# Splitting the copy of the selected key blocks between ScalarE and VectorE in a hybrid decoder step

## What is computed

```python
k_full = cache_k[page_table[:, :own_first]].astype(f32).reshape(Bd, n_full, MOBA_BLOCK, H, D)
kmean = jnp.mean(k_full, axis=2)
gate = jnp.einsum('bhtd,bnhd->bhtn', qf, kmean)
_, sel = lax.top_k(gate, topk)                      # 3 of 16 blocks, for each of 8 heads
...
s = jnp.einsum('bhtd,bhtkd->bhtk', qf, kg.astype(f32)) * scale
scores.append(s - slopes * (tpos[None, None, :, None] - kpos).astype(f32))
...
p = jax.nn.softmax(jnp.concatenate(scores, axis=-1), axis=-1)
```

## Time and profile before

| what | us |
|---|---|
| median of 3 runs | 459.38 |
| lowest and highest | 459.01 and 478.45 |
| the profiled execution's own time | 457.99 |
| span of the profile | 456.4 |

### The profile page before, as it was taken

The page is one execution under the profiler, slowest core; times in us unless marked ns, Lnnn a source line. Parts: engine busy times, 40 slices in busy tenths (PEclk is TensorE's granted clock), DMA queues, the critical chain, the costliest instruction groups (busy, mean ns, idle before and its releaser), DMA issues.

```text
span 456.4 us, 8864 instructions
## 1 busy us (share of the span) xinstructions
PE 402.1 (88%) x2696; PEld 189.5 (42%) x2696; DVE 278.8 (61%) x756; ACT 125.2 (27%) x282; POOL 244.7 (54%) x347
## 2 busy tenths in 40 slices
PE   4896997998779999899998897989999388999993
PEld 2543442433343444344553354434443253334433
DVE  2443167447624569666966884868865796567432
ACT  2310120000012223554547522362435401000101
POOL 4776305556446506563377745882566556667121
PEclk9897998999979999899999998999999769999999
DMA  8999158996799936997499849975699599945311
GB/s 223 408 390 337 49 183 227 363 328 164 202 382 331 254 105 190 361 320 185 117 336 318 241 127 333 327 202 156 210 368 337 162 362 378 343 103 117 115 46 52
DMA packets 79695, 111.26 MB, mean 244 GB/s; under 512 B 46560, under 2 KB 47584, under 8 KB 79648
## 3 DMA queue, kind: packets, MB, share of 16 engines
q0 software_dynamic: 22576, 71.45, 46.4%
q1 hardware_dynamic: 45280, 21.26, 18.3%
q10 hardware_dynamic: 11792, 17.98, 13.2%
HBM read 106.34 MB, written 4.29 MB: 242 GB/s over the span
## 4 chain that ended last, share of the span: by engine, by line
PE 27%; DMA 25%; issue 13%; POOL 10%; DVE 9%; SPq 7%; another core or an unknown queue 4%; DVEq 2%; POOLq 2%; ACT 1%
DMA K<-in_cache_k,kidx 20%; PE PA L1036 12%; POOL K L899 8%; PE PA L1142 7%; SPq L777 4%; DVE ksum L1619 4%; DMA V<-in_cache_v 2%; PE SB L990 2%; PE GB L1159 2%; DMA V<-in_page_table 2%; PE DC L1188 1%; DVEq L1617 1%; POOLq L726 1%; SPq L780 1%
## 5 line engine op out<-in xcount | busy, mean ns | idle before, releaser
L899 POOL DMA_INDIRECT K<-in_cache_k,kidx x128 | 135.5, 1059 | 135.3 <-DVE ksum L1619 69.2
L1036 PE MATMUL PA<-wbuf,hT 128*128 128x512 f32 x384 | 187.8, 623 | 4.5 <-ACT vn L1302 2.6
L744 DVE TENSOR_TENSOR ksum<-K 128x512 f32<-128x512 f32 x128 | 86.5, 689 | 74.7 <-DMA K<-in_cache_k,kidx 54.4
L1036 PEld LDWEIGHTS PA<-wbuf,hT 128*128 128x128 f32 x384 | 69.4, 196 | 82.1 <-issue 73.3
L729 POOL DMA_DIRECT2D V<-in_cache_v x128 | 76.2, 595 | 33.8 <-issue 26.1
L1142 PE MATMUL PA<-wbuf,hT 128*128 128x512 f32 x128 | 59.6, 606 | 0.0
L1619 DVE TENSOR_TENSOR ksum<-K,qb 128x128 f32<-128x128 f32 x192 | 41.8, 287 | 10.9 <-issue 4.3
L1159 PE MATMUL GB<-ksum,win 128*32 128x512 f32 x256 | 34.1, 604 | 5.0 <-DVE ksum L744 4.7
L1142 PEld LDWEIGHTS PA<-wbuf,hT 128*128 128x128 f32 x128 | 23.1, 192 | 25.7 <-issue 25.2
L1036 PE MATMUL PA<-hT,wbuf 128*128 128x512 f32 x64 | 31.0, 630 | 0.0
L990 PE MATMUL SB<-wbuf,hTs 128*32 128x128 f32 x576 | 22.0, 305 | 6.7 <-DMA wbuf<-in_w_in 3.7
(11 more groups left out here) (200 smaller groups left out, 363.5 us busy)
## 6 DMA issues: line engine op xcount, KB each, us to landing
wbuf<-in_w_in ACTq DMA_DIRECT2D x20, 512.0 KB
V<-in_cache_v SPq DMA_DIRECT2D x240, 32.0 KB
V<-in_cache_v POOLq DMA_DIRECT2D x128, 32.0 KB, 2.8
wbuf<-in_w_out ACTq DMA_DIRECT2D x8, 512.0 KB
wbuf<-in_w_in SPq DMA_DIRECT2D x8, 256.0 KB, 8.6
K<-in_cache_k,kidx POOLq DMA_INDIRECT x128, 7.8
wbuf<-in_w_in SPq DMA_DIRECT2D x4, 512.0 KB
qb<-q_rows SPq DMA_DIRECT2D x8, 256.0 KB
```

Source lines behind the costliest of these rows:

```text
L744: eng.tensor_tensor(ksum[:, n % SUMS, :], K[:, n, 0, :], K[:, n, 1, :], ALU.add).then_inc(s_dsum, 1)
L899: pool.indirect_dma_start(K[:, n, :, :].rearrange("p r w -> p (r w)"), None, k_rows, bass.IndirectOffsetOnAxis(ap=kidx[:, b, n:n + 1], axis=0)
L1036: last = pe.matmul(bank[:, :], lhs, rhs, start=(kc == 0), stop=(kc == KC - 1))
```

## The change

ScalarE gets a new step "ex", with the highest priority in its plan. It waits for `s_sel`, loads eight registers, and copies the eight blocks of rank one from `K` to `kq` without a product. It raises `s_exa`. VectorE keeps the 16 products of ranks two and three, in four parts of four. Then a new VectorE step "em" waits for `s_exa` and multiplies the eight copies in place by q, as one instruction of 128 partitions x 8 x 128 elements, and raises `s_exm`. `K` is free when both `s_ext` and `s_exa` are up; the q row's buffer `qb` is free when both `s_ext` and `s_exm` are up. The costs in the plan change with it, and `MARGIN` goes from 0.6 to 1.0.

```diff
-PARTS = 4
+PARTS, BY_ACT = 4, 8
...
-            deps = [("DVE", ("ex", b - 1, PARTS - 1))] if b else []
+            deps = [("DVE", ("ex", b - 1, PARTS - 1)), ("ACT", ("ex", b - 1))] if b else []
...
-            add("DVE", "gate", s, {"ex": 1.7, "pg": 1.2, "sr": 3.4}[s[0]], *deps)
+            if s[0] == "em":
+                deps.append(("ACT", ("ex", b)))
+            add("DVE", "gate", s, {"ex": 1.15, "pg": 1.2, "em": 1.2, "sr": 3.4}[s[0]], *deps)
+        add("ACT", "copyk", ("ex", b), 3.1, ("DVE", ("pg", b)))
...
-            add("SP", "spread", ("qb", b), 3.0, ("DVE", ("ex", b - 1, PARTS - 1)))
+            add("SP", "spread", ("qb", b), 3.0, ("DVE", ("em", b - 1)))
...
-TILE_US, KEY_US, LAG, MARGIN, SLACK, QUARTERS = 7.4, 1.65, 0.25, 0.6, 0.05, 8
+TILE_US, KEY_US, LAG, MARGIN, SLACK, QUARTERS = 7.4, 1.65, 0.25, 1.0, 0.05, 8
...
                     if b >= 1 and n == 0:
                         pool.wait_ge(s_ext, b)
+                        pool.wait_ge(s_exa, b)
...
+                elif kind == "ex":
+                    b = s[1]
+                    act.wait_ge(s_sel, b + 1)
+                    if b >= 1:
+                        act.wait_ge(s_scr, b)
+                    for x in range(BY_ACT):
+                        k, h = divmod(x, H)
+                        if h == 0:
+                            block_regs = [act.alloc_register(f"ablk{b}_{k}_{i}") for i in range(H)]
+                            act.load(block_regs, selT[k:k + 1, b % 2, 0:H])
+                        n = act.snap(block_regs[h], min_val=0, max_val=NB - 1)
+                        last = act.copy(kq[:, h * TOP + k, :, :],
+                                        K[:, bass.ds(n, 1), :, h * HD:(h + 1) * HD].rearrange("p a r d -> p (a r) d"))
...
+                    last.then_inc(s_exa, 1)
...
-                    size = H * TOP // PARTS
-                    for x in range(size * part, size * (part + 1)):
+                    size = (H * TOP - BY_ACT) // PARTS
+                    for x in range(BY_ACT + size * part, BY_ACT + size * (part + 1)):
...
+                elif kind == "em":
+                    b = s[1]
+                    dve.wait_ge(s_exa, b + 1)
...
+                        last = dve.tensor_tensor(by_rank[:, k, 0:hs, :, :], by_rank[:, k, 0:hs, :, :],
+                                                 q_heads[:, 0:hs, :].unsqueeze(2).broadcast_to([P, hs, 2, HD]),
+                                                 ALU.mult)
+                    last.then_inc(s_exm, 1)
                 elif kind == "sr":
                     b = s[1]
                     dve.wait_ge(s_ext, b + 1)
+                    dve.wait_ge(s_exm, b + 1)
```

More of the change, by code:

```diff
@@ L63, in add @@
         needs[eng, s] = deps
-    for eng, names in (("PE", "gate score first attention side sample project"), ("ACT", "weight square score exp turn sample side evacuate squares fetch"),
+    for eng, names in (("PE", "gate score first attention side sample project"), ("ACT", "copyk weight square score exp turn sample side evacuate squares fetch"),
                        ("DVE", "first " + DVE_LANES), ("POOL", POOL_LANES), ("SP", "spread rows fetch gather"),
@@ L270, in make_plan @@
         parts = [("ex", b, i) for i in range(PARTS)]
-        for s in ([("pg", b)] + parts if b == B - 1 else parts[:1] + [("pg", b)] + parts[1:]) + [("sr", b)]:
+        for s in ([("pg", b)] + parts if b == B - 1 else parts[:1] + [("pg", b)] + parts[1:]) + [("em", b), ("sr", b)]:
             deps = [("ACT", ("mb", b - 1))] if s[0] == "sr" and b else []
-            add("DVE", "gate", s, {"ex": 1.7, "pg": 1.2, "sr": 3.4}[s[0]], *deps)
+            if s[0] == "em":
+                deps.append(("ACT", ("ex", b)))
+            add("DVE", "gate", s, {"ex": 1.15, "pg": 1.2, "em": 1.2, "sr": 3.4}[s[0]], *deps)
+        add("ACT", "copyk", ("ex", b), 3.1, ("DVE", ("pg", b)))
         if b:
-            add("SP", "spread", ("qb", b), 3.0, ("DVE", ("ex", b - 1, PARTS - 1)))
+            add("SP", "spread", ("qb", b), 3.0, ("DVE", ("em", b - 1)))
         add("PE", "score", ("bc", b), 0.4, ("DVE", ("pg", b)), ("DVE", ("sr", b)))
@@ L592, in hymba_kernel @@
         s_scr = sem("selected_k_scored")
+        s_exa = sem("selected_k_copied")
+        s_exm = sem("copied_k_times_q")
         s_mxr = sem("decode_max_ready")
@@ L823, in _ @@
                         sp.wait_ge(s_ext, b)
+                        sp.wait_ge(s_exm, b)
                     sp.dma_start(qb[:, :], q_rows[b:b + 1, :].broadcast_to([P, W])).then_inc(s_qb, 16)
@@ L1353, in _ @@
                     fetch_v(act, b, hh, [k], "va")
+                elif kind == "ex":
[11 more added lines that the diff above has]
+                                        K[:, bass.ds(n, 1), :, h * HD:(h + 1) * HD].rearrange("p a r d -> p (a r) d"))
+                        if h == H - 1 or x == BY_ACT - 1:
+                            for r in block_regs:
+                                act.free_register(r)
+                    last.then_inc(s_exa, 1)
                 elif kind == "mb":
@@ L1628, in _ @@
                         last.then_inc(s_ext, 1)
+                elif kind == "em":
+                    b = s[1]
+                    dve.wait_ge(s_exa, b + 1)
+                    by_rank = kq[:, :, :, :].rearrange("p (h k) r d -> p k h r d", k=TOP)
+                    q_heads = qb[:, :].rearrange("p (h d) -> p h d", h=H)
+                    for k in range(-(-BY_ACT // H)):
+                        hs = min(H, BY_ACT - k * H)
+                        last = dve.tensor_tensor(by_rank[:, k, 0:hs, :, :], by_rank[:, k, 0:hs, :, :],
+                                                 q_heads[:, 0:hs, :].unsqueeze(2).broadcast_to([P, hs, 2, HD]),
+                                                 ALU.mult)
+                    last.then_inc(s_exm, 1)
                 elif kind == "sr":
```

2 lines of the change are left out of this document (1 added, 1 removed).

## The result

The changed kernel took 470.91 us (median of 4 runs, 469.13 to 475.71), the kernel before 460.03 beside it (459.01 to 478.45). The ratio is 1.026, with a 95% interval of 1.016 to 1.036. The forecast was 458.5 us, 446 to 467, with 12% for slower: the result lies outside. Single executions of either kernel scatter by 3% and more, and the ratios leave the disturbed ones out.

A forecast was written before the change was run, and what follows sets the result against it. TensorE and the key cycle were taken as two bounds within a few us. Terms -4.7 + 6.2 + 1.5 - 4.0 = -1.0 us took 457.99 to 457.0; 1.4 for the runs' median gave 458.4, rounded to 458.5, range 446 to 467.

The forecast's parts named there:

- The gaps: From each sequence's gate to the next first gather: 1.75 us shorter, or 0.7 at worst.
- The load stage as a constant: Sixteen gathers of a sequence, first to last: 25.0 us, taken as fixed within the key cycle of 46.3 us.
- ScalarE's hold: ScalarE held until 9.4 us after the gate, delaying copies out of TensorE's banks: costed at nothing, at worst 1 us a sequence.
- The tail: Time behind the last gate, 52.6 us before: longer by more TensorE steps (+6.2 us) and a later end (+1.5).
- seven more steps: TensorE behind the last gate: 47 projection steps against 40, +6.2 us.
- the longer end: Behind TensorE's last sample product: squaring, scaling and storing the prompt's last tile, +1.5 us (0 to 3).
- `MARGIN` gives back 4.0 us: TensorE's waits for key sums (4.7 us) and in one score step (4.2): larger `MARGIN` takes back 4 of 8.9 us.
- The stretches by numbers of steps: Stretches between gates, costed by TensorE's moved projection and attention steps and the keys' pace: -4.7 us to the last gate.
- The last stretch: Stretch to gate 7: output projection from about 21 us, 46 to 47 us against 48.2, so -1.5 us.
- B: Rival: the order costs more than the keys give; last gate no earlier, longer tail paid in full, 467 us; chance 0.13.
- C: Rival: ScalarE comes late with the copies, each delay moving the next load; 470 us, slower; chance 0.10.
- A: Rival: the key cycle sets the pace, so seven gaps each 1.75 us shorter count in full; 447 us; chance 0.22.

The follow-up runs named there:

- e2: Changed kernel's order with ScalarE's copies and "em" struck out, VectorE making all 24 products again; 477.49 us, ratio 1.030 to the kernel before.
- e1: Kernel before, its order kept, with only ScalarE's copies and "em" put in; 457.35 us against 463.96, ratio 0.987.
- e15: The kernel of e1 run once more, in five rounds; 461.90 us against 463.58 for the kernel before.
- e5: Changed kernel with only the four residual loads issued later, after the last sequence's gathers are issued; 467.81 us, ratio 1.010 to the kernel before.
- e8: The kernel of e1 with the four residual loads issued later, as in e5; 458.95 us against 465.95 for the kernel before.
- e9: Changed kernel with each weight chunk's four quarter loads issued together and the residual loads late; 466.80 us, ratio 1.009 to the kernel before.
- e16: The kernel of e1 with weight loads drawn together as in e9, but residual loads at their first place; two times, 458.42 and 472.67 us.
- e13: The changed kernel run again, nothing altered; 470.21 us against 463.58 for the kernel before, ratio 1.030.
- e3: Kernel before with only `MARGIN` raised from 0.6 to 1.0; 475.51 us against 463.96.
- e4: Changed kernel with `MARGIN` put back from 1.0 to 0.6; 494.75 us, ratio 1.071 to the kernel before.

## Why the prediction was wrong, point by point

- **The gaps: right.** Forecast 1.75 us less per sequence, the first gather 9.6 to 10.6 us after the gate. Measured -12.5 us in seven, 1.8 each, and 9.6 to 10.2 us in six of the seven gaps; the gap ahead of sequence 6 was 11.2 and 12.4 (13.2 and 13.0 before). The time of a copy (294 ns, forecast 0.30) and of "em" (1.22 us, forecast 1.23) were right too; only the copies overlap more than assumed.
- **The load stage as a constant: this step failed.** I took 25.0 us for every sequence out of one stretch and carried it over ("46.3 - 1.8 = 44.5"). It has no such value: it depends on what other queues move beside it. The rows for that stood in the trace of before, as the last stage took 26.5 us (367.66 to 394.13) with 3.3 MB beside it. I had costed ScalarE's hold as a matter of TensorE's banks, "at nothing", and forgot that the queue behind the copies holds the weight loads: of a step that holds an engine, every DMA behind it counts. Nor did I look where the new order puts the loads. The stages came to 26.9 us on the mean instead of 25.0: 13.6 us in seven, more than the whole gain, of which the order alone makes 5.7 (e2) and the copies alone 5 to 9 (e1, e15). So the key cycle that I put at 44.5 us stayed at 46.8 (10.2 + 26.9 + 9.7), where it had been. For the last stage (+5.8) e5, e8, e9 and e16 show that the bytes are the cause; for the other six (+7.8) it is the likely one.
- **The tail: right in kind, too large in size.** The terms were seven more steps (+6.2) and the longer end (+1.5), 7.7 us together; measured are +5.5, 58.1 and 58.0 us. TensorE's last product ends 51.1 us behind the gate instead of 46.3 (+4.8), and what follows takes 7.0 us instead of 6.3 (+0.6). The shorter gap does not show here: with the copies alone the tail is 52.5 us (e1), with the order alone 58.1 (e2).
- **`MARGIN` gives back 4.0 us: not so.** TensorE's wait for key sums, 4.7 us in the earlier trace rows, is 9.3 in the changed kernel and 7.5 in e13, and its waits for ScalarE's copy-out, 4.2 us there, are 5.0 and 4.0. In the kernel before the larger margin costs 11.5 us (e3), with the copies the smaller one costs about 24 (e4 against the changed kernel). I had priced a planner's constant by the waits it is aimed at; it reorders all, and has no sign of its own.
- **The stretches by numbers of steps:** to the last gate I had -4.7 and -4.0 us. The means of the last gate are 409.9 in both kernels, (403.8 + 415.9) / 2 and (411.5 + 408.3) / 2: nothing, as well as two profiles that lie 12 us apart can tell. The step counts for stretches 3 and 4 (-4.7, -2.1) did not show as time; the stretches took +2.0 and +1.3 in the first pair of profiles.
- **The last stretch:** forecast 46 to 47 us with the projection from 21 us on; it began at 23.5 and the stretch took 52.1. The idle time was foreseen "as long again" as before; it grew from 12.4 to 18.8 us, and of the two score waits 5.9 us hang on late keys.
- **The rivals.** B came true in its consequence, the last gate no earlier and a longer tail (7.7 us by its price of 467, 5.5 measured), by another way than the stalls I gave it. C and A did not: the gaps gave what was forecast, only the one ahead of sequence 6 was over 11 us, and the last gate is far from 393.

Put right, the sum comes near: with 0 in place of the 4.7 us at the last gate and 0 in place of the 4.0 of the margin, the forecast would have been 458.5 + 8.7 = 467.2, against 470.9 and 470.2. With the measured 5.5 us for the tail in place of 7.7 it would have been 465.0. No part accounts for the 5 to 6 us that remain; they lie within what the kernel before itself moved from chip to chip (medians of 460.0 to 466.0, where the forecast took 459.4).

Open is what makes the idle times without a releaser, on TensorE in chains of small products and on VectorE and ScalarE for 4 to 15 us, in single cases more, most of them while gathers run (ScalarE has one or two of 6 to 7 us behind the last gate as well). No run took the gathers away from such a place. Open is too how the changed costs and `MARGIN` together came to put seven steps more behind the last key sums.

No version beats the kernel before for certain. The best is the copies in the old order: 0.987 (0.975 to 0.999) in e1, 461.9 against 463.6 in e15.

## What to carry to other kernels

Where a new step makes an engine wait, list what stands behind it on that engine's queue, transfers above all, and ask where in the traffic they now begin: here copies that ended just as the gathers began, together with a new order, sent 21 loads out beside them instead of 3, and the whole gain was given back. Test a change of work and a change of order apart, by editing the finished order; a planner's constant or cost changes the order everywhere, and its effect can't be read from the wait that it is aimed at. And split two profiles of the same kernel before explaining a part of one: here one part differed by 17 us with nothing changed.

## What was not expected of the hardware

- Copies on ScalarE out of SBUF take 294 ns each by their own row, but follow each other by (1.10 - 0.29) / 4 = 0.20 us: eight end within 1.7 us. The forecast of eight times 0.30 was 0.7 us too long.
- 2 MB beside 6.4 MB of gathers in flight cost 3.8 us (e5) and 4.2 us (e16) of load stage, while all queues together moved 324 GB/s without and 356 with them: at 356 GB/s the added 2.2 MB of e16 take 6.3 us, and the gathers lost two thirds of that.
- A chain of small float32 products on TensorE took 6.1 or 20.0 us in two executions of the same program, while gathers ran.
